# RWKV scan on one Trainium2 core: each 128x128 block-diagonal product as two 64x64 products

## The reference

```python
def step(S, inp):                      # per head, S is 64x64
    r_t, w_t, k_t, v_t, kk_t, b_t = inp
    sa = einsum('bhij,bhj->bhi', S, -kk_t)
    S = (S * w_t[:, :, None, :] + sa[..., None] * b_t[:, :, None, :]
         + v_t[..., None] * k_t[:, :, None, :])
    return S, einsum('bhij,bhj->bhi', S, r_t)
y = rwkv7_scan(..., False) + rwkv7_scan(..., True)
```

## Time and profile before

| what | value |
|---|---|
| time, median of 3 runs | 3702.26 us (3701.38 to 3710.27) |
| the profiled execution | 3707.42 us, span 3705.7 us |
| mean granted TensorE clock over the span | 0.936 of full |
| the scan: from the first load of vectors to the last update of the state | 2465.85 to 2913.3 us of the span |

### The profile page before, as it was taken

One profiled execution on the slowest core, in us unless ns is written; L12 is line 12 of the kernel. 1 busy time (PEld: TensorE's weight loads), 2 busy tenths in 40 slices (PEclk: granted clock), 3 DMA queues, 4 the chain that ended last, 5 costly groups with the idle time before them and its releaser, 6 DMA issues. The chain is left out here.

```text
span 3705.7 us, 45830 instructions
## 1 busy us (share of the span) xinstructions
PE 3254.9 (88%) x16116; PEld 2681.0 (72%) x16116; DVE 1880.1 (51%) x2666; ACT 1121.1 (30%) x1832; POOL 1576.2 (43%) x963
## 2 busy tenths in 40 slices
PE   6966889999999999999999997819999777799977
PEld 4854657888888888777878884519999566488755
DVE  2035338965777770577777773453333554333114
ACT  2334222333333332211111113413333333333222
POOL 4430344454444443444444443236655333344433
PEclk8988988999999999999999998959999888799988
DMA  2210121344454546455555541240110020122221
GB/s 104 96 51 0 46 80 63 114 144 128 158 202 161 186 171 223 158 190 184 188 181 190 184 160 40 87 131 16 30 30 16 6 68 24 40 96 97 95 85 57
DMA packets 165873, 396.14 MB, mean 107 GB/s; under 512 B 53008, under 2 KB 53136, under 8 KB 164112
## 3 DMA queue, kind: packets, MB, share of 16 engines
q1 hardware_dynamic: 165776, 394.78, 32.9%
HBM read 314.77 MB, written 79.95 MB: 107 GB/s over the span
## 5 line engine op out<-in xcount | busy, mean ns | idle before, releaser
L158 POOL TENSOR_TENSOR weights_low<-weights_raw,weights_high 128x1024 fp32r<-128x1024 f32 x435 | 1134.9, 2609 | 1412.1 <-ACT weights_high L150 1412.1
L150 ACT ACTIVATE weights_high<-weights_raw 128x1024 fp32r<-128x1024 f32 x435 | 461.2, 1060 | 1954.1 <-PE psum L233 1848.0
L231 PE MATMUL psum<-expert_in_high,weights_high 128*128 128x512 f32 x1152 | 462.2, 401 | 21.6 <-POOL expert_in_low L327 10.5
L232 PE MATMUL psum<-expert_in_low,weights_high 128*128 128x512 f32 x1152 | 452.4, 393 | 0.0
L233 PE MATMUL psum<-expert_in_high,weights_low 128*128 128x512 f32 x1152 | 452.3, 393 | 0.0
L231 PE MATMUL psum<-coefficients_high,weights_high 128*128 128x512 f32 x1024 | 400.0, 391 | 17.1 <-DVE coefficients_low L1058 15.4
L233 PE MATMUL psum<-coefficients_high,weights_low 128*128 128x512 f32 x1024 | 398.6, 389 | 0.0
L232 PE MATMUL psum<-coefficients_low,weights_high 128*128 128x512 f32 x1024 | 398.5, 389 | 0.0
L1058 DVE TENSOR_TENSOR coefficients_low<-activation_in,coefficients_high 128x512 fp32r<-128x512 f32 x128 | 306.4, 2394 | 4.4
L231 PEld LDWEIGHTS psum<-expert_in_high,weights_high 128*128 128x128 f32 x1152 | 218.7, 190 | 72.1 <-issue 9.8
L233 PEld LDWEIGHTS psum<-expert_in_high,weights_low 128*128 128x128 f32 x1152 | 218.5, 190 | 46.2
(11 more groups left out here) (391 smaller groups left out, 5824.0 us busy)
## 6 DMA issues: line engine op xcount, KB each, us to landing
weights_raw<-in_weights SPq DMA_DIRECT2D x437, 512.0 KB, 3.6
expert_activations<-expert_activation SPq DMA_DIRECT2D x128, 256.0 KB, 4.2
coefficient_table<-table_stage SPq DMA_DIRECT2D x8, 4096.0 KB, 13.3
table_group<-coefficient_table SPq DMA_DIRECT2D x16, 2048.0 KB, 11.6
activation_in<-expert_activations SPq DMA_DIRECT2D x128, 256.0 KB, 3.8
chunk_vectors<-scan_vectors SPq DMA_DIRECT2D x8, 1280.0 KB, 8.2
scan_vectors<-scan_stage SPq DMA_DIRECT2D x8, 1024.0 KB, 4.1
residual_stream<-in_x SPq DMA_DIRECT2D x1, 2048.0 KB, 7.4
```

Of the source, the lines that this page charges most:

```text
L150: act.activation(d.hi[:, m % SPLIT, :], d.raw[:, m % RAW, :], ACT.Copy).then_inc(d.high, 1)
L158: pool.tensor_tensor(d.lo[:, m % SPLIT, :], d.raw[:, m % RAW, :], d.hi[:, m % SPLIT, :].bitcast(F32), ALU.subtract).then_inc(d.split, 1)
L231: pe.matmul(acc, w[0][:, cols], x[0], start=start, stop=False)
L232: pe.matmul(acc, w[0][:, cols], x[1], start=False, stop=False)
```

## The change

Each product is now two matmuls, one per head: `HALVES` are the partitions 0 to 63 and 64 to 127, and each matmul takes stationary operand, moving operand and output from one half, [64, 64] weights with moving width 64 (128 for the scores). No tile is block-diagonal any more; `bd`, `wb`, `sab`, `Sb`, `vc` and all zeroing but that of `S` are gone, and there is one form of everything. The transposes are now products with a 64x64 identity (`eye2`), b and k together in one bank. ACT makes one copy of each product, DVE works on 64 columns per unit everywhere, POOL only masks the levels, on all 128 partitions at once. DVE and POOL loop 8 times over one chunk; ACT's loop is as before; PE has no loop: its eight chunks are written out.

```diff
+    HALVES = (slice(0, C), slice(C, 2 * C))
-        bd = sb("block_diagonal_vectors", [P, 2, 4, U, P])
-        bt, kt, vt = sb("b_by_token", [P, U, P]), sb("k_by_token", [P, U, P]), sb("v_by_token", [P, U, P])
-        vc = sb("v_compact", [P, U, C])
+        bkt = sb("b_and_k_by_token", [P, 2, U, C])
+        vt = sb("v_by_token", [P, U, C])
-        lk = sb("k_a_products", [P, U, P])
-        bl = sb("L_level", [P, 2, U, P])
-        wc, wb = sb("W_compact", [P, U, C]), sb("W_block_diagonal", [P, U, P])
-        X, XT = sb("X_compact", [P, U, C]), sb("X_transposed", [P, U, P])
+        lk = sb("k_a_products", [P, U, C])
+        bl = sb("L_level", [P, 2, U, C])
+        w = sb("L_level_times_X", [P, U, C])
+        X, XT = sb("X", [P, U, C]), sb("X_transposed", [P, U, C])
...
-                Bank(k, "rwkv", 4 * g + 2, [("b_t", 1), ("v_t", 1)] + [(f"dXT{l}", 1) for l in lv[1:]] + [("S", 1)]),
-                Bank(k, "rwkv", 4 * g + 3, [("k_t", 1), ("rhs", 1)])]
+                Bank(k, "rwkv", 4 * g + 2, [("v_t", 1)] + [(f"dXT{l}", 1) for l in lv[1:]] + [("S", 1)]),
+                Bank(k, "rwkv", 4 * g + 3, [("bk_t", 1), ("rhs", 1)])]
...
             def _(pool):
-                for t in (bd, lk, bl, wb, sab, Sb, S):
-                    pool.memset(t[tuple([slice(None)] * len(t.shape))], 0.0).then_inc(zeroed, 1)
-                pool.wait_ge(zeroed, 7)
...
+                pool.memset(S[:, :, :], 0.0).then_inc(zeroed, 1)
+
+                with pool.Fori(0, NCH) as i:
+                    for l in range(LV):
                         for g in range(2):
...
+                            m = consts("levels")[:, None, l * C:(l + 1) * C].to_broadcast([P, H, C])
+                            pool.tensor_tensor(bl[:, l % 2, half(g), :], L[:, half(g), :], m, ALU.mult).then_inc(lev[g], 1)
...
-                with pe.Fori(0, NCH // 2) as ii:
-                    for n in range(2):
-                        i = ii * 2 + n
+                for i in range(NCH):
+                    n = i % 2
+
+                    def product(g, b, name, width, terms, at=0, last=True):
+
+                        bank = banks[g][b]
+                        if at == 0:
                             bank.free(pe, i, name)
...
+                        for u in range(H):
+                            cols = slice(at + u * width, at + (u + 1) * width)
+                            for j, (lhs, rhs) in enumerate(terms):
+                                for r in HALVES:
+                                    mm = pe.matmul(bank.ps[r, cols], lhs(r, g * H + u), rhs(r, g * H + u),
+                                                   start=(j == 0), stop=(j == len(terms) - 1))
+                        if last:
                             mm.then_inc(bank.made, 1)
...
+                    pe.wait_ge(cb_in[n], i // 2 * 16 + 16)
+                    for g in range(2):
+                        product(g, 0, "scores_b", P, [(vec(2), a_and_r)])
+                        product(g, 1, "scores_k", P, [(vec(3), a_and_r)])
+                    for g in range(2):
+                        product(g, 3, "bk_t", C, [(vec(2), eye)], last=False)
+                        product(g, 3, "bk_t", C, [(vec(3), eye)], at=H * C)
+                    for g in range(2):
+                        product(g, 2, "v_t", C, [(vec(4), eye)])
...
+                            if l < LV - 1:
+                                product(g, 1, f"dX{l}", C, [(of(XT), of(w))])
+                            product(g, 2, f"dXT{l}", C, [(of(w), of(XT))])
...
+                    for g in range(2):
+                        banks[g][0].taken(pe, i, "sa")
+                        product(g, 1, "y", C, [(of(S), vec(1)), (of(sa), of(mb)), (of(vt), of(mk))])
+                        product(g, 2, "S", C, [(lambda r, u: bkt[r, 0, u, :], of(sa)),
+                                               (lambda r, u: bkt[r, 1, u, :], of(vt))])
...
             def _(act):
-                act.wait_ge(zeroed, 7)
-
-                def both_forms(g, src, compact, block_diagonal):
-                    act.activation(compact[:, half(g), :], src, ACT.Copy)
-                    for hh in range(2):
-                        r = slice(hh * C, hh * C + C)
-                        ins = act.activation(block_diagonal[r, half(g), r], src[r, :, :], ACT.Copy)
-                    ins.then_inc(banks[g][0].read, 1)
...
                         for l in range(1, LV):
                             for g in range(2):
...
-                                both_forms(g, src, wc, wb)
+                                take(g, 0, f"W{l}", w[:, half(g), :], view(g, 0, C))
...
-                dve.wait_ge(zeroed, 7)
-                with dve.Fori(0, NCH // 2) as ii:
-                    for n in range(2):
-                        i = ii * 2 + n
+                dve.wait_ge(zeroed, 1)
+                with dve.Fori(0, NCH) as i:
...
-                                dve.tensor_tensor(XT[:, half(g), :], view(g, 2, P), XT[:, half(g), :],
-                                                  ALU.add).then_inc(banks[g][2].read, 1)
+                            dve.tensor_tensor(XT[:, half(g), :], view(g, 2, C), XT[:, half(g), :],
+                                              ALU.add).then_inc(banks[g][2].read, 1)
```

More of the change, by code:

```diff
@@ L1721, in half, with view @@
             return slice(g * H, g * H + H)
+        def view(g, b, width):
+            return banks[g][b].ps[:, 0:H * width].rearrange("p (u t) -> p u t", u=H)
         with nc.Block() as block:
@@ L1891, in _ @@
-                            act.activation(vt[:, half(g), :], src, ACT.Copy)
-                            for hh in range(2):
-                                r = slice(hh * C, hh * C + C)
-                                ins = act.activation(vc[r, half(g), :], src[r, :, r], ACT.Copy)
-                            ins.then_inc(bank.read, 1)
+                            take(g, 2, "v_t", vt[:, half(g), :], view(g, 2, C))
                         for l in range(1, LV):
                             for g in range(2):
-                                bank = banks[g][0]
-                                bank.full(act, i, f"W{l}")
-                                src = bank.ps[:, 0:H * C].rearrange("p (u t) -> p u t", u=H)
-                                both_forms(g, src, wc, wb)
+                                take(g, 0, f"W{l}", w[:, half(g), :], view(g, 0, C))
@@ L1902, in _ @@
                         for g in range(2):
-                            take(g, 3, "rhs", rr[:, half(g), :], C)
+                            take(g, 3, "rhs", rr[:, half(g), :], view(g, 3, C))
                         for g in range(2):
-                            banks[g][0].full(act, i, "sa")
-                            both_forms(g, banks[g][0].ps[:, 0:H * C].rearrange("p (u t) -> p u t", u=H), sa, sab)
+                            take(g, 0, "sa", sa[:, half(g), :], view(g, 0, C))
                         for g in range(2):
-                            bank = banks[g][1]
@@ L1909, in _ @@
-                            bank.full(act, i, "y")
-                            act.activation(ys[:, half(g), bass.ds(i * C, C)],
-                                           bank.ps[:, 0:H * C].rearrange("p (u t) -> p u t", u=H),
-                                           ACT.Copy).then_inc(bank.read, 1)
+                            take(g, 1, "y", ys[:, half(g), bass.ds(i * C, C)], view(g, 1, C))
             @block.vector
@@ L1962, in _ @@
                                 if l == 1:
[L1963 removed]
+                                    banks[g][0].taken(dve, i, "W0")
                                 else:
[L1965 to L1975 removed]
+                                    banks[g][1].taken(dve, i, f"dX{l - 1}")
@@ new lines, in _ @@
+                                dve.tensor_tensor(X[:, half(g), :], view(g, 1, C), X[:, half(g), :],
+                                                  ALU.add).then_inc(banks[g][1].read, 1)
+                            banks[g][2].full(dve, i, f"dXT{l}")
+                            if l == 1:
+                                dve.wait_ge(ready[g], i + 1)
+                            else:
+                                banks[g][2].taken(dve, i, f"dXT{l - 1}")
+                            dve.tensor_tensor(XT[:, half(g), :], view(g, 2, C), XT[:, half(g), :],
+                                              ALU.add).then_inc(banks[g][2].read, 1)
@@ new lines, in _ @@
+                    for g in range(2):
+                        bank = banks[g][2]
+                        bank.full(dve, i, "S")
+                        dve.tensor_tensor(S[:, half(g), :], view(g, 2, C), S[:, half(g), :], ALU.add).then_inc(chain[g], 1)
+                        dve.wait_ge(chain[g], i + 1)
+                        dve.tensor_tensor(S[:, half(g), :], S[:, half(g), :],
+                                          ends[:, half(g), bass.ds(i, 1)].to_broadcast([P, H, C]),
+                                          ALU.mult).then_inc(bank.read, 1)
```

224 lines of the change are left out of this document (67 added, 157 removed).

## The result

The changed kernel takes 3498.0 us (median of 4 runs, 3496.7 to 3503.5) where the one before takes 3704.7 beside it: a ratio of 0.944, interval 0.943 to 0.946, 207 us saved. Forecast were 3542 us and a range of 3500 to 3710. The profiled execution took 3498.97 us, its span is 3497.2.

The account below looks back on a forecast made before the run. PE was taken to bound the scan, by weight loads or instructions per record. Eight chunks of 34.3 us, 3 for the start and 1.3 for the last state update gave 278.7 against 438.9, so 3542 us, range 3500 to 3710.

Parts of the forecast that it names:

- p = 0.034: PE's time per matmul record in the changed scan, in us, chosen a fifth above 0.028; gives chunks of 34.3 us.
- The prediction's best case: PE's records: half the columns halve the load and both heads run at once, 0.028 us each, a chunk 30.0 us.
- The round trip: A product's way from PE through another engine and back: 0.88 us through ACT, 0.92 through DVE.
- The start on the lower clock: Scan's beginning with PE at the lower granted clock: 3 us added to the sum.
- the chunk's formula: One chunk of the scan on PE: 9.8 + 720p us, p being the time per record; 34.3 us predicted.
- Taking turns: Rival: the two halves on PE don't overlap, 0.056 us per record, runs 3669 or 3698 us; chance 0.25.
- The full price: Rival: each smaller PE record still costs 0.112 us, +368 us, runs 4070 us; chance 0.20.
- Supply: Rival: PE's written-out program isn't supplied fast enough, 42 to 154 us of stops, 3584 to 3696 us; chance 0.09.
- POOL's masking on 128 partitions: POOL's 12 maskings per chunk: 0.76 us each, between 0.76 and 1.5, fitting into a level of 3.6 us.
- its cover: Loop turns of DVE and POOL at chunk ends: hidden behind PE by 1.2 us; uncovered up to 15 us.
- The loop's turns: PE's three loop turns in the kernel before, removed by unrolling: 3 x 6.8 = 20 us at most.
- The copies: ACT's half-partition copies, about half of its work, go; said to pay only because PE waited 0.2 us for each.

Follow-up runs that it names:

- e3: Changed kernel with each product's matmuls reordered, all of one half first, then all of the other: 3567.4 us, ratio 0.963, a chunk 39.1 us.
- e1: Changed kernel with PE back in its loop of four turns and a separate semaphore increment ahead of each product: 3595.9 us, ratio 0.971, scan 318.3 us.
- e1c: Changed kernel with one separate increment of an unused semaphore on PE ahead of each of the 304 products: 3540.7 us, ratio 0.956, scan 293.2 us.
- e11: Changed kernel with the lower half's products computed twice and the upper half's left out: 4073.8 us, scan 820.5 us.
- e12: Changed kernel with an already satisfied semaphore wait on PE ahead of each product: 3502.7 us, scan 254.8 us.
- e6: Changed kernel with POOL's maskings split into 64 partitions at a time, 24 per chunk instead of 12: 3495.5 us, ratio 0.941, scan 248.6 us.
- e2: Kernel before the change with only PE's loop written out: 3707.3 us, ratio 1.001, scan 433.1 us.
- e5: Changed kernel with ACT copying each `W` three times, once on 128 partitions and twice on 64: 3526.5 us, ratio 0.950, scan 275.4 us.
- e4: Changed kernel with all products of partitions 64 to 127 left out: 3675.1 us, scan 412.2 us.
- e8: Changed kernel with 16 more records, loading and moving 32 columns, ahead of each `dX`: 3535.5 us, scan 273.8 us.
- e13: Changed kernel with the vector loads from the third chunk on shrunk to one partition's 64 elements: 3487.8 us, scan 241.9 us.

## Why the prediction was right about the way and wrong about the size

**The step that failed** is the choice of p = 0.034, "a fifth above the best", with the reason that both passes of one head stand ahead of the other head's, "so the pairing can't be perfect". The pairing is perfect as far as can be measured: 0.0292 a record, 0.058 a pair, against 0.059 for one half's record alone at the same clock (e3). A chunk has 720 such terms, so this is 8 x 720 x 0.0048 = 27.6 us of the miss. The prediction's best case, 0.028, was right to 4%; the price of a record was bounded from the right rows, and the value in between was chosen without one.

**The round trip** was put at 0.88 us through ACT and 0.92 through DVE, and is 0.69. The end of a matmul lies 0.19 beyond its pace and not 0.25 (a 64x64 record lasts 0.218 us where the 128x128 one lasted 0.275), and from the copy to PE pass 0.06 us and not 0.20. Seven round trips a chunk, 0.2 shorter each, are some 11 us of the scan. The start on the lower clock was put at 3 us and cost 5.5 - 3.4 = 2.1. Against them stand two things that were not in the sum: `W1` waits for DVE's `X` in both groups and not in one (3.6 us, of which the sum has about half), and two late packets (1.7 us).

**The sum.** From the landing at 2467.4 to the last state update the scan took 243.8 us, 278.7 were predicted: 34.9 less. By the chunk's formula with 0.0292 and 0.69 a chunk is 29.4 us; it is 29.85. Outside the scan the profiled execution was 13.4 us shorter than that of before, and it lay 1.0 and not 5.2 us above the median: 3547.2 - 34.9 - 13.4 = 3498.9. Whether those 13.4 us belong to the change stays open. That part varies by 28 us over the profiles above, and not only by chance: e1 exceeds e1c there by 28 us, and by 55 us in the medians of times that don't overlap, with 25 us in the scan. The three kernels with 128x128 operands have 3252 to 3259 us there, the others at most 3253 but for e1 (3258), down to 3231. No run separates what makes it. A range for this kernel needs that spread, and mine had none at its low end. With p at 0.028 my own sum gives 3508; the scan came out at exactly that end (243.8 against 244.3), by luck in part, since a p too small by 0.0012 (7 us) and round trips too long by 0.19 (11 us) nearly cancel there, and the part outside it went past.

**The rivals.** Taking turns (3669 to 3698 us) is excluded by the 0.0289 us of the row at 2592.27; e3 shows what part of it would have come with another order. The full price (4070) is excluded by the same row. e11 comes out at that time (4073.8) by another way, at the lower clock and in one half. The Trainium skill ("TensorEngine Tiling (Array Packing)", Restrictions and Gotchas) says that different row tiles can't access the same PSUM bank simultaneously; the runs here disagree, at least for halves that differ in rows and in columns: both write one bank in every product, and a pair takes 0.058 us where one record alone takes 0.059 at the same clock. Supply (3584 to 3696) was given 0.09 because there was no wait on issue "at a third of the rate" in straight code, which says little about three times that. It costs 1.7 us here, but e12 and e1c show that it is close: 2% more instructions make it 11.

**Costs put at little or nothing.** POOL's masking on 128 partitions at 0.76 us was right (0.74), and its cover held (e6). DVE's and POOL's loops show no cost: PE has no wait for POOL in the scan. The start went as forecast: PE's first record is at 2467.57, 0.1 us after the landing. The loop's turns, counted as 20 us at most from the first alone, cost 17 in the kernel before, are worth 25 in the compact kernel (e1 - e1c) and nothing in the block-diagonal one by itself (e2), because a wait of POOL's came in their place and took the clock with it. The copies of which I wrote that they pay "only because PE waited 0.2 us for each" are worth 32 us in the new kernel (e5): what was nearly hidden behind PE at 0.112 us per record is on the path at 0.029.

## What to carry to other kernels

Block-diagonal operands pay for their zeros: a record with 128 columns of weights took 0.111 us though only 64 moved, where a pair with 64 and 64 takes 0.058; the scores, which move 128 columns, gained next to nothing (0.107 a pair after 0.113). Where heads are at most 64 wide and move no more, give each half of the array its own product and alternate the halves record by record, since half by half a chunk takes 39 us instead of 30. When PE becomes this quick, look next at the round trips through the other engines and at the supply of PE's program, and keep instructions that only touch semaphores out of its stream. An estimate that has a best case from rows and no row for the deviation should take the best case as its value, or put it well inside the range.

## What the runs showed of the hardware

- With one quarter of the array in use from start to end, PE busy for 320 of 320 us was granted 1.2 GHz (e4), also with as many records as the changed kernel has (e11); with two quarters in use it was granted 2.4 GHz (1.00 from 2474 to 2704 in the changed kernel), also where up to 24 records of one half follow each other (e3).
- Two records in different halves take the time of one: 0.058 us a pair, 0.059 one alone, both at a granted clock of 1.00 and with one PSUM bank for both.
- The time of an fp32 record pair goes by the larger of the columns loaded and moved: 0.032 us for 32, 0.058 for 64, 0.107 for 128. A change of shape adds about 0.09 (e8).
- Matmuls of different halves start out of program order: in e3's rows a record of `W` (2599.86) starts ahead of a record of the `dXT` that stands before it in the program (2599.91). The Trainium skill ("TensorE: Matmul & The Clock Gate", Part 3) says that matmuls start and end in program order; this trace disagrees for halves with rows and columns of their own.
- A written-out program on PE at 0.029 us a record is fed by packets of about 250 loads and matmuls (57 in the scan); 125 records at 0.0292 us are 3.7 us, so one is needed every 3.7 us where PE does not wait (an estimate from these two numbers). The loads of the vectors delay them: two gaps of 0.74 and 1.13 us with them, none without (e13), in one profile each.
- A semaphore increment by itself on PE costs 0.16 us on the mean (49.6 / 304), some 37 of the 49.6 us in gaps that look like late packets, the rest with five stretches at 1.2 GHz among it and not taken apart; riding on a matmul it costs nothing that can be measured (243.7 against 243.6 us).
